# A two-block transformer on one core: the up products of the first block's feed-forward layers read unnormalized activations, and the norm's factor is applied at read-out

## The reference, cut to what matters

```python
D_FF = ((8 * D_MODEL // 3 + 63) // 64) * 64      # 2752 in the reference's formula, 22 tiles of 128 in the kernel
def rmsnorm(x, g):
    y = xf * lax.rsqrt(jnp.mean(xf * xf, axis=-1, keepdims=True) + EPS)
    return (y * g.astype(jnp.float32)).astype(x.dtype)
def conv_ffn(x, w_up, conv_w, w_down):
    u = causal_dwconv(x @ w_up, conv_w)           # three taps along the tokens, one weight per feature and tap
    gate, val = jnp.split(u, 2, axis=-1)
    return (jax.nn.silu(gate) * val) @ w_down
# in each of the two layers of the first block:
        h = h + rmsnorm(mix, g[1])
        ff = conv_ffn(rmsnorm(h, g[2]), ffn_w_up[l], ffn_conv[l], ffn_w_down[l])
        h = h + rmsnorm(ff, g[3])
```

## Time and profile before

| | |
|---|---|
| runs, us | 1592.5, 1583.23, 1590.25 (median 1590.25) |
| profiled execution | its span is 1589.5 us, which is also all that the profile tells of its time |
| TensorE busy | 1464.9 us, 92% |
| VectorE busy | 1043.3 us, 66% |
| ScalarE busy | 780.4 us, 49% |
| GpSimd busy | 282.3 us, 18% |
| matmuls of `up0` and `up1` | 3 groups of 704, some 285 to 290 ns each, overlapping |

### The profile page before, as it was taken

How to read it: one execution, slowest core, us unless ns; L and a number is a source line. 1 busy time by engine, 2 the same in 40 slices (tenths; PEclk the granted TensorE clock), 3 DMA queues, 4 the chain that set the end, 5 groups by cost and what they waited for, 6 DMA issues and landing times. The chain is left out here.

```text
span 1589.5 us, 29025 instructions
## 1 busy us (share of the span) xinstructions
PE 1464.9 (92%) x11301; PEld 1401.3 (88%) x11301; DVE 1043.3 (66%) x1727; ACT 780.4 (49%) x1272; POOL 282.3 (18%) x384
## 2 busy tenths in 40 slices
PE   5999879999787998999997899989999988999997
PEld 4999779999686767899996799989999987899997
DVE  5664677886765444788867754357787666687643
ACT  5655645454354444455445564664443555554341
POOL 0000102120054420111100153202333100123110
PEclk9999999999898988999997999999999999999999
DMA  7433525659432112455781321135776634365451
GB/s 283 182 114 110 203 101 215 221 188 344 169 143 96 54 54 106 151 220 205 294 316 72 138 76 54 54 106 205 272 261 228 225 119 156 106 260 217 143 182 46
DMA packets 41140, 265.80 MB, mean 167 GB/s; under 512 B 4560, under 2 KB 5712, under 8 KB 15440
## 3 DMA queue, kind: packets, MB, share of 16 engines
q1 hardware_dynamic: 41040, 264.44, 45.9%
HBM read 263.38 MB, written 1.05 MB: 166 GB/s over the span
## 5 line engine op out<-in xcount | busy, mean ns | idle before, releaser
L224 DVE TENSOR_TENSOR w_lo<-raw,w_hi 128x2048 fp32r<-128x2048 f32 (+2 forms) x207 | 426.4, 2065 | 235.9 <-ACT w_hi L220 232.0
L220 ACT ACTIVATE w_hi<-raw 128x2048 fp32r<-128x2048 f32 (+3 forms) x224 | 385.8, 1727 | 37.2 <-PE bank L414 33.1
L412 PE MATMUL bank<-x_hi_up,w_hi 128*128 128x272 f32 (+1 forms) x704 | 203.8, 290 | 8.1 <-DVE x_lo_up L717 8.1
L414 PE MATMUL bank<-x_hi_up,w_lo 128*128 128x272 f32 (+1 forms) x704 | 202.1, 287 | 0.0
L413 PE MATMUL bank<-x_lo_up,w_hi 128*128 128x272 f32 (+1 forms) x704 | 201.6, 286 | 0.0
L412 PE MATMUL bank<-z_hi,w_hi 128*128 128x258 f32 x704 | 200.3, 285 | 0.0
L413 PE MATMUL bank<-z_lo,w_hi 128*128 128x258 f32 x704 | 198.7, 282 | 0.0
L414 PE MATMUL bank<-z_hi,w_lo 128*128 128x258 f32 x704 | 198.0, 281 | 0.0
L412 PEld LDWEIGHTS bank<-x_hi_up,w_hi 128*128 128x128 f32 x704 | 133.7, 190 | 9.8 <-issue 8.8
L413 PEld LDWEIGHTS bank<-x_lo_up,w_hi 128*128 128x128 f32 x704 | 134.2, 191 | 0.0
L414 PEld LDWEIGHTS bank<-x_hi_up,w_lo 128*128 128x128 f32 x704 | 133.8, 190 | 0.0
(11 more groups left out here) (461 smaller groups left out, 3898.6 us busy)
## 6 DMA issues: line engine op xcount, KB each, us to landing
raw<-w_up SPq DMA_DIRECT2D x44, 1024.0 KB, 4.8
raw<-w_gu SPq DMA_DIRECT2D x44, 1024.0 KB, 4.8
work<-w_ada SPq DMA_DIRECT2D x27, 1024.0 KB, 5.0
raw<-w_down SPq DMA_DIRECT2D x32, 704.0 KB, 5.0
raw<-w_dn SPq DMA_DIRECT2D x32, 704.0 KB, 4.2
raw<-w_a_in SPq DMA_DIRECT2D x16, 1024.0 KB, 5.5
mod_w_down<-w_ada SPq DMA_DIRECT2D x16, 1024.0 KB, 6.3
raw<-w_gdn_qkv SPq DMA_DIRECT2D x12, 1024.0 KB, 4.8
```

Source lines behind the costliest of these rows:

```text
L220: act.activation(w_hi[:, s, 0:blocks * P], raw[:, s, 0:blocks * P], ACT.Copy).then_inc(hi_split.sem, 1)
L224: dve.tensor_tensor(w_lo[:, s, 0:blocks * P], raw[:, s, 0:blocks * P], w_hi[:, s, 0:blocks * P].bitcast(F32), ALU.subtract).then_inc(lo_sp ...
L412: pe.matmul(o, w_hi[:, s, b], x_hi[:, xk, cols[0]:cols[1]], start=begin, stop=False)
L414: last = pe.matmul(o, w_lo[:, s, b], x_hi[:, xk, cols[0]:cols[1]], start=False, stop=end)
```

## The change

Both layers of the first block are changed alike, in five parts.

1. The entry (`BranchEntry`) no longer normalizes before the split. As soon as a tile of `h` is complete, ScalarE makes `x_hi` from `h` times the gain and VectorE `x_lo`; the factor 1/rms, which is one number per column, is left out. The second root's sum of squares is gathered by GpSimd in `std`, one tile after the other; one matmul with ones follows in place of eight.
2. TensorE takes items 0 and 1 together (`first_two`, `paired`): tile k of item 0 with tile k-2 of item 1. The root's matmul is issued before item 1's last tile, and with it comes the second root and inverse (`root`).
3. The item's two tiles lie in one of four pairs of banks, for up and down products (`groups=4`). Item j waits for the read-out of item j-4; items 2 to 5 wait at least for that of item 0.
4. Read-out: VectorE multiplies both tiles by 1/rms (`z`, one buffer per tile, L994 after). ScalarE makes tap 2 (`conv`, L1005) and tap 1 (`tap1`, L1007) from `z`, GpSimd adds these two (L1034), VectorE adds tap 0 (`dve_conv`, L1014), at the head of `dve_late`, behind the splits.
5. In the first item, too, the weight splits come first (`early`).

```diff
+                    if halves and groups == 4:
+                        return bank[4 + ((s - first) % SLOTS) // 2]
...
+                    if groups == 4:
+                        return bank[2 * ((s - first) % SLOTS) + t]
...
-                        early = not act_late or isinstance(r, int) and r == first + n - 1
+                        early = not act_late or isinstance(r, int) and (r == first + n - 1 or paired and r == first)
...
+                    def first_two():
+                        lag = 2
+                        pe.wait_ge(lo_split.sem, first + 1)
+                        for m in range(k_tiles + lag):
+                            if m == lag:
+                                pe.wait_ge(lo_split.sem, first + 2)
+                            if m < k_tiles:
+                                pe.wait_ge(entry.split.sem, entry.split.at(m + 1))
+                            for i, kk in ((0, m), (1, m - lag)):
+                                if not 0 <= kk < k_tiles:
+                                    continue
+                                s = (first + i) % SLOTS
+                                for t in range(tiles):
+                                    o = where(first + i, s, t)[:, 0:width]
+                                    b = slice((t * k_tiles + kk) * P, (t * k_tiles + kk + 1) * P)
+                                    pe.matmul(o, w_hi[:, s, b], x_hi[:, kk, cols[0]:cols[1]], start=kk == 0, stop=False)
+                                    pe.matmul(o, w_hi[:, s, b], x_lo[:, kk, cols[0]:cols[1]], start=False, stop=False)
+                                    last = pe.matmul(o, w_lo[:, s, b], x_hi[:, kk, cols[0]:cols[1]], start=False,
+                                                     stop=kk == k_tiles - 1)
+                                if kk == k_tiles - 1:
+                                    last.then_inc(item_done.sem, 1)
+                            if m == k_tiles:
+                                root.pe_root(pe)
...
+                        if groups == 4 and not halves:
+                            pe.wait_ge(item_out.sem, max(i - 3, first + 1) if isinstance(i, int) else i - 3)
...
-                            pe.wait_ge(item_out.sem, i - 1)
+                            pe.wait_ge(item_out.sem, first - 3 if groups == 4 else i - 1)
...
+                def act(act):
+                    act.activation(std[:, c0:c1], bank[7][:, 0:width], ACT.Sqrt, scale=1.0 / D,
+                                   bias=eps_col[:, 0:1]).then_inc(std_made.sem, 1)
+                    for k in range(KD):
+                        act.wait_ge(h_added.sem, h_added.at(k + 1))
+                        act.activation(x_hi[:, k, c0:c1], h[:, k, c0:c1], ACT.Copy, scale=gain(k)).then_inc(x_high.sem, 1)
+                        act.activation(work[:, k, c0:c1], h[:, k, c0:c1], ACT.Square).then_inc(squared.sem, 1)
...
+                def act_root(act):
+                    act.wait_ge(summed.sem, summed.at(1))
+                    act.activation(std[:, c0:c1], bank[7][:, 0:width], ACT.Sqrt, scale=1.0 / D,
+                                   bias=eps_col[:, 0:1]).then_inc(std_made.sem, 1)
...
+                def dve(dve):
+                    def weigh(k):
+                        dve.scalar_tensor_tensor(work[:, k, c0:c1], work[:, k, c0:c1], weight(k), rstd[:, c0:c1],
+                                                 ALU.mult, ALU.mult).then_inc(weighed.sem, 1)
+
+                    def add(k):
+                        dve.wait_ge(weighed.sem, weighed.at(k + 1))
+                        dve.tensor_tensor(h[:, k, c0:c1], h[:, k, c0:c1], work[:, k, c0:c1], ALU.add).then_inc(h_added.sem, 1)
+
+                    def low(k):
+                        dve.wait_ge(x_high.sem, x_high.at(k + 1))
+                        dve.scalar_tensor_tensor(x_lo[:, k, c0:c1], h[:, k, c0:c1], gain(k), x_hi[:, k, c0:c1].bitcast(F32),
+                                                 ALU.mult, ALU.subtract).then_inc(x_split.sem, 1)
+                    invert(dve, 1)
+                    weigh(0)
+                    add(0)
+                    for k in range(1, KD):
+                        weigh(k)
+                        low(k - 1)
+                        add(k)
+                    low(KD - 1)
+
...
+                def pe_root(pe):
+                    pe.wait_ge(gathered.sem, gathered.at(KD))
+                    pe.matmul(bank[7][:, 0:width], ones, total, start=True, stop=True).then_inc(summed.sem, 1)
...
+            def dve_out(dve, j, s, where):
+                item_ready(dve, up, j)
+                if not isinstance(j, int) or j >= 1:
+                    dve.wait_ge(tapped.sem, tapped.at(j * 4))
+                    dve.wait_ge(conved.sem, conved.at(j * 2))
+                for t in range(2):
+                    dve.tensor_tensor(z[:, t, :], where(t)[:, 0:width_in], rstd[:, c0:c1], ALU.mult).then_inc(z_made.sem, 1)
+                dve.wait_ge(z_made.sem, z_made.at(j * 2 + 2))
+                dve.sem_inc(item_out.sem, 1)
...
+                for t in range(2):
+                    act.wait_ge(z_made.sem, z_made.at(j * 2 + (t + 1)))
+                    if t == 0 and (not isinstance(j, int) or j >= 1):
+                        act.wait_ge(added.sem, added.at(j * 2))
+                    if t == 0 and (not isinstance(j, int) or j >= 2):
+                        act.wait_ge(multiplied.sem, multiplied.at(j - 1))
+                    act.activation(conv[:, s % 2, t, :], z[:, t, lead:width_in], ACT.Copy,
+                                   scale=weight(j, 2, t)).then_inc(tapped.sem, 1)
+                    act.activation(tap1[:, t, skip(1):width], z[:, t, lead + skip(1) - 1:width_in - 1], ACT.Copy,
+                                   scale=weight(j, 1, t)).then_inc(tapped.sem, 1)
+
+            def dve_conv(dve, j, s, where):
+                for t in range(2):
+                    dve.wait_ge(added.sem, added.at(j * 2 + (t + 1)))
+                    d = conv[:, s % 2, t, skip(2):width]
+                    dve.scalar_tensor_tensor(d, z[:, t, lead + skip(2) - 2:width_in - 2], weight(j, 0, t), d, ALU.mult,
+                                             ALU.add).then_inc(conved.sem, 1)
             def act_late(act, j, s, where):
+                act.wait_ge(conved.sem, conved.at(j * 2 + 1))
+                act.activation(act_s[:, s % 2, :], conv[:, s % 2, 0, :], ACT.Silu).then_inc(silued.sem, 1)
...
             def dve_late(dve, j, s, where):
+                dve_conv(dve, j, s, where)
                 dve.wait_ge(silued.sem, silued.at(j + 1))
...
-                src = value[:, s % 2, :] if conv else where(1)[:, 0:width]
-                dve.tensor_tensor(prod[:, s % 2, :], act_s[:, s % 2, :], src, ALU.mult).then_inc(multiplied.sem, 1)
...
             def pool_out(pool, j, s):
-
+                for t in range(2):
+                    pool.wait_ge(tapped.sem, tapped.at(j * 4 + (2 * t + 2)))
+                    d = conv[:, s % 2, t, skip(1):width]
+                    pool.tensor_tensor(d, d, tap1[:, t, skip(1):width], ALU.add).then_inc(added.sem, 1)
                 pool.wait_ge(multiplied.sem, multiplied.at(j + 1))
...
+            return Product(up, 2, KD, x_hi, x_lo, cols, act_out=act_out, dve_out=dve_out, pool_out=pool_out,
+                           act_late=act_late, dve_late=dve_late, entry=entry, root=entry, paired=True, groups=4,
+                           room=one_room, room_ready=(entry.gathered, KD),
...
-            return Product(down, 1, HALF_FF, a_hi, a_lo, (0, out[1] - out[0]), halves=True, sums=out, sqrt_next=True,
+            return Product(down, 1, HALF_FF, a_hi, a_lo, (0, out[1] - out[0]), halves=True, groups=4, sums=out, sqrt_next=True,
```

More of the change, by code:

```diff
@@ L860, in fused_model, with up_product @@
         gain1 = lambda layer, i: (lambda k: par("gains", (4 * layer + i) * KD + k))
-        def up_product(layer, x_hi, x_lo, a_hi, a_lo, cols, up, conv, phase, entry):
-            lead = 0 if cols[0] == 0 else CONV_LEAD * conv
+        def up_product(layer, x_hi, x_lo, a_hi, a_lo, cols, up, phase, entry):
+            lead = 0 if cols[0] == 0 else CONV_LEAD
             width_in = cols[1] - cols[0]
             width = width_in - lead
-            gate = sbuf(phase, f"gate_{up}", [P, 2, width])
-            value = sbuf(phase, f"value_{up}", [P, 2, width])
+            c0, c1 = cols
+            z = sbuf(phase, f"z_{up}", [P, 2, width_in])
+            tap1 = sbuf(phase, f"tap1_{up}", [P, 2, width])
+            conv = sbuf(phase, f"conv_{up}", [P, 2, 2, width])
@@ L873, in up_product @@
             first, n, _ = starts[up]
-            taps = 4 if conv else 0
-            def act_out(act, j, s, where):
-                item_ready(act, up, j)
-                if not conv:
-                    return
-                if not isinstance(j, int) or j >= 2:
-                    act.wait_ge(multiplied.sem, multiplied.at(j - 1))
-                for t, dst in ((0, gate), (1, value)):
```

(33 more changed lines are left out.)

66 lines of the change are left out of this document (45 added, 21 removed).

## The result

The changed kernel takes 1696.28 us (median of 4 runs, 1694.08 to 1697.93) against 1589.17 (1583.23 to 1592.5): 1.0684 times as long, 95% interval 1.0665 to 1.0703. The forecast was 1666, with a range to 1692, so the time lies outside it. The direction and the place were right, the loss was 106 us in the profiled executions (spans of 1695.6 and 1589.5) and not 76.

What follows compares the result with a forecast made beforehand. TensorE's matmuls set the pace before; after the change the ring would. Layer 0 loses 36.5 us and layer 1 39.0, entry gains included: 1589.5 + 75.5 = 1665.0, forecast 1666 us, range 1638 to 1692.

Steps and rivals of the forecast that it cites:

- The ring: Up steps: handovers between ScalarE and VectorE form a loop of 7.24 or 7.38 us, above TensorE's 5.73 and 6.00.
- rival A: Up products: TensorE's pace still decides, only the entry counts, less about 1 us for a later end; 1577 us, chance 0.04.
- The columns: Up items 1, 5, 9, 13, 17, 21: modulation columns, 2.49 us between `w_lo` and last tap, no longer hidden.
- Rival B: Up products: the modulation columns stay hidden as in the trace, 25 us less, 1641 us; chance 0.05.
- The turn: One up item from `z` to next `z`, four copies at 0.33 or 0.35 included: 7.24 us at 258 columns, 7.38 at 272.
- The register loop: In 12 of the 22 up steps handovers take longer: 0.15 us a turn in all, between 0 and 0.5.
- The entry: Start of each layer's up product: a tile costs 1.35 us; gain 6.4 us in layer 0, about 7.5 in layer 1.
- The last item: End of the up product: step 21's start to GpSimd's second half 8.6 us in layer 0, second down item 0.7 later.
- GpSimd's adds cost nothing: Up steps: both new adds end 2.9 us into a turn, 3 us before the last tap wants them.
- Rival C: Up steps: GpSimd's adds fall beside `w_lo` and end after it, 1.5 us more in 40 turns, 1725 us; chance 0.05.
- Rival D: Up products: TensorE stays at the lower clock, 12 us an item in place of 6, about 1810 us; chance 0.02.
- The waits: Both up products: TensorE waits for `w_lo` about 1.4 us for most items, 3.9 every fourth, some 70 in all.

Runs made afterwards that it cites:

- experiment 1: Changed kernel with ScalarE's weight split of item j+3 ahead of item j's copies in every up step, VectorE's order kept: 1640.16 us, 1.0337 of the kernel before.
- experiment 3: Changed kernel with VectorE's last tap (both tiles) moved ahead of its `w_lo`, ScalarE's order kept: 1653.25 us, 1.0417 of the kernel before.
- experiment 4: Changed kernel with an up item's modulation columns ahead of VectorE's split instead of behind it: 1673.93 us, 1.0533 of the kernel before.
- experiment 10: Changed kernel with ScalarE's split first, tap 1 by VectorE, taps, Silu and product one item behind, `z` doubled, entry squares summed by TensorE: 1601.62 us, 1.0076.
- experiment 5: Changed kernel with ScalarE's four copies a step made without the weights of taps 1 and 2: 1676.28 us, 1.0568 of the kernel before.
- experiment 6: Changed kernel with all 22 steps of both up products written out, none in the register loop: 1685.84 us, 1.0612 of the kernel before.
- experiment 7: Changed kernel with GpSimd's eight steps of the entry's sum of squares replaced by one copy at the end: 1689.31 us, 1.0632 of the kernel before.
- experiment 8: Changed kernel with tap 1 by VectorE, without ScalarE's copies for it and GpSimd's adds, split order as changed: 1694.69 us, 1.0665 of the kernel before.
- experiment 11: Kernel of experiment 10 with tap 1 on ScalarE's two copies and GpSimd's two adds again: 1610.51 us, 1.0129 of the kernel before.

## Why the prediction was right in its sign and short in its size

- **The ring: shown.** It was forecast from the order of the waits against two sums (4.1 and 4.4 us an item) that spoke for rival A. The turn is 7.63, and the reordering of instructions alone gave back 56, 43 and 22 us (experiments 1, 3, 4). Rival A fails at its condition: no full turn came under 5.7 in the changed kernel. Its price was wrong too: in experiment 10, where TensorE hardly waits for `w_lo`, the end of the product still costs 7.6 and 9.6 us, where A had "about 1 us" in all.
- **The columns: shown.** A column turn is 2.5 us longer, and experiment 4 returns 22 us of my 25 for ten turns. Rival B is out.
- **The turn: mis-sized.** The step that failed is "four copies at 0.33 from start to start", 0.35 at 272 columns. They are 0.41 apart, since they carry a column of scales and the rows that I priced them by did not. That is 0.25 us in 40 turns, 10 us of the 30.6 missed. Taking the scales away gave 20 us in experiment 5, more than its 0.38 a turn accounts for (some 16). My own terms add up to 7.40 at 272 columns, not 7.38, which is 0.4 us.
- **The register loop: mis-sized.** I took 3.6 us for both layers (0.15 a turn); experiment 6 shows 10.
- **The entry: one cost left out.** "Then a tile costs ... 1.35 us" had GpSimd's gathering at nothing. That the two engines can hold each other stood in the prediction, with a cast of 1.62 in place of 0.40, but it was weighed for the adds of the turn alone. GpSimd held VectorE's add to `h`; experiment 7 shows 7 us for both layers.
- **The last item: short by 1.5 us a layer, and its follower by as much.** 8.6 us were forecast from step 21's start to GpSimd's second half; it took 10.1, columns and adds stretching each other. ScalarE then read the down item 2.2 us later, not 0.7, behind a table load and two splits.
- **Layer by layer**, at ScalarE's read of the second down item: layer 0 lost 49.7 us (50.2, with 0.5 there already at 199) and layer 1 54.3, for forecasts of 36.5 and 39.0. Of these 28.5 us of miss the terms above make up 27: 10 for the copies, 6 for the loop, 5 for the entry up to `z` of item 0, 6 for the last items. Between the two layers 3.7 us came back and behind them 5.1 were added, for which no experiment was made.
- **GpSimd's adds cost nothing: right in the turn** (experiment 8), wrong in the last step. Rival C's mechanism is real, but needs another order (experiments 1 and 11).
- **Rival D: out.** The mean clock is 0.95, and after each stretch at the lower level it came back (0.54, then 1.00 from 283 on).
- **The waits: near by luck.** 63.5 us for `w_lo` stand against "some 70", but in 27 waits and not in nearly every item, and for a larger loss. The stretches at the lower clock filled the rest of the ring's time, as the rows at 0.54 and 0.50 show; they are a part of the 26 us that TensorE's busy time grew by.

## What to carry to other kernels

Each engine's work per item says how fast a pipeline could go; the longest loop of "waits for" and "stands behind" over the engines says how fast it goes. Sum that loop with rows of exactly the instruction form that is added, give the last item's chain a sum of its own, and ask of each GpSimd instruction what VectorE does in that moment. An order that costs nothing while TensorE sets the pace (columns, gathering, adds) is part of the price once it does not.

## What the runs showed of the hardware

- VectorE and GpSimd hold each other, in both directions. VectorE's add took 1.00 for 0.43 beside a GpSimd add, two taps 1.72 for 0.91, a split 2.86 for 2.29, a modulation column 1.78 for 1.22; two GpSimd adds took 2.79 beside a split and 4.59 beside a column and a split for 1.59. The Trainium skill ("SBUF — State Buffer", Who interferes with whom) has a VectorE instruction with two SBUF inputs and a reading GpSimd instruction exclude each other, whichever comes first holding the other; the trace agrees.
- An activation with a scale per partition took 0.52 us at 272 columns, without it 0.43, and the following one began 0.41 or 0.32 later.
- TensorE's granted clock fell to the lower level (1.2 GHz, 0.50) after waits of 2.05 and 4.26 us inside the product and was at 1.00 again some 4 us later. While other engines set the pace, this lengthened TensorE's busy time and shortened its next wait.
